# Queries and B's keys turned on VectorE in 32x32 blocks over all 128 rows, and carried between partition quarters by DMA

## The reference

```python
for l in range(DEPTH):                      # 2 layers
    x = x + 0.5 * _swiglu(_rmsnorm(x, ffn1_norm[l]), ...)
    h = _rmsnorm(x, mix_norm[l])
    a_q, a_kv, i_q, i_k, i_w, b_qkv, c_q, c_kv, c_g, m_g = jnp.split(h @ w_in[l], cuts, axis=-1)
    # rope on a_q, a_k, i_q, i_k, b_q, b_k, c_q (also used unrotated), k_slc, k_win
    # A: attention over the keys picked by the indexer (i_q, i_k, i_w)
    # B: causal attention with own keys for each of its 4 heads
    # C: 8 heads in 2 groups: compressed, selected (S) and window (W) attention, gated
    # the three branches, gated by m_g, are summed and go through w_out
    x = x + 0.5 * _swiglu(_rmsnorm(x, ffn2_norm[l]), ...)
return _rmsnorm(x, final_norm)
```

## Time and profile before

| | |
|---|---|
| median of 3 runs | 1163.5 us (1162.96 to 1163.73) |
| the profiled execution | 1163.91 us |
| its span, first to last instruction | 1162.2 us |
| TensorE busy | 1153.9 us (99% of the span) |
| VectorE busy | 951.5 us (82%) |
| ScalarE busy | 581.7 us (50%) |
| GpSimd busy | 31.9 us (3%) |
| turns on TensorE, line 1546 | 68 |
| block turns on VectorE, line 693 | 64, 19.4 us |
| granted TensorE clock | 0.998 of full speed |

### The profile page before, as it was taken

One profiled execution on the slowest core, in us unless ns is written; L12 is line 12 of the kernel. 1 busy time (PEld: TensorE's weight loads), 2 busy tenths in 40 slices (PEclk: granted clock), 3 DMA queues, 4 the chain that ended last, 5 costly groups with the idle time before them and its releaser, 6 DMA issues.

```text
span 1162.2 us, 16328 instructions
## 1 busy us (share of the span) xinstructions
PE 1153.9 (99%) x5573; PEld 945.9 (81%) x5573; DVE 951.5 (82%) x1788; ACT 581.7 (50%) x757; POOL 31.9 (3%) x67
## 2 busy tenths in 40 slices
PE   9999999999999999999999999999999999999997
PEld 7888888887778888888888888888877788888886
DVE  6877788899977687778887887878999696888777
ACT  6444345447764464344454444454578635434433
POOL 2000000001000000000000000000010000000000
PEclk9999999999999999999999999999999999999999
DMA  8566554765425555655556556556653335655561
GB/s 285 190 214 216 181 188 163 234 203 163 137 80 182 181 157 204 217 191 185 195 177 202 180 173 215 182 189 191 198 180 110 141 135 184 219 181 169 202 234 38
DMA packets 148996, 211.04 MB, mean 182 GB/s; under 512 B 8160, under 2 KB 109136, under 8 KB 148944
## 3 DMA queue, kind: packets, MB, share of 16 engines
q1 hardware_dynamic: 148256, 209.64, 54.5%
q10 hardware_dynamic: 688, 0.71, 0.2%
HBM read 209.28 MB, written 1.05 MB: 181 GB/s over the span
## 4 chain that ended last, share of the span: by engine, by line
PE 99%; DVE 0%; issue 0%; ACT 0%; POOLq 0%; POOL 0%; DVEq 0%
PE ps L1371 30%; PE ps L1373 30%; PE ps L1372 30%; PE ps L1585 2%; PE ps L1421 1%; PE ps L1641 1%; PE ps L1613 1%; PE ps L1390 1%; PE ps L1546 1%; PE ps L1558 0%; PE ps L1765 0%; PE ps L1672 0%; PE ps L1632 0%; DVE x L1000 0%; PE ps L1573 0%
## 5 line engine op out<-in xcount | busy, mean ns | idle before, releaser
L1114 ACT ACTIVATE whi<-raw 128x2048 fp32r<-128x2048 f32 (+1 forms) x195 | 365.9, 1879 | 253.3 <-PE ps L1373 252.2
L536 DVE TENSOR_TENSOR wlo<-raw,whi 128x2048 fp32r<-128x2048 f32 (+1 forms) x195 | 433.9, 2244 | 65.6 <-ACT whi L1114 45.7
L1371 PE MATMUL ps<-whi,ht_hi 128*128 128x512 f32 (+1 forms) x1192 | 465.6, 391 | 0.2
L1373 PE MATMUL ps<-whi,ht_lo 128*128 128x512 f32 (+1 forms) x1192 | 460.8, 387 | 0.0
L1372 PE MATMUL ps<-wlo,ht_hi 128*128 128x512 f32 (+1 forms) x1192 | 460.3, 386 | 0.0
L1373 PEld LDWEIGHTS ps<-whi,ht_lo 128*128 128x128 f32 x1192 | 223.9, 188 | 45.9
L1371 PEld LDWEIGHTS ps<-whi,ht_hi 128*128 128x128 f32 x1192 | 224.0, 188 | 45.0 <-issue 1.4
L1372 PEld LDWEIGHTS ps<-wlo,ht_hi 128*128 128x128 f32 x1192 | 224.1, 188 | 43.9
L598 DVE STREAM_TRANSPOSE scr<-scr 32x128 f32<-32x128 f32 x688 | 208.3, 303 | 10.3
L1371 PE MATMUL ps<-whi,at_hi 128*128 128x512 f32 x304 | 118.5, 390 | 0.0
L1372 PE MATMUL ps<-wlo,at_hi 128*128 128x512 f32 x304 | 118.3, 389 | 0.0
(11 more groups left out here) (176 smaller groups left out, 757.3 us busy)
## 6 DMA issues: line engine op xcount, KB each, us to landing
raw<-in_ffn_w_down_dram SPq DMA_DIRECT2D x88, 512.0 KB, 4.9
raw<-in_w_in_dram SPq DMA_DIRECT2D x88, 512.0 KB, 4.5
raw<-in_ffn_w_gate_dram SPq DMA_DIRECT2D x85, 512.0 KB, 4.0
raw<-in_ffn_w_up_dram SPq DMA_DIRECT2D x85, 512.0 KB, 5.0
raw<-in_w_out_dram SPq DMA_DIRECT2D x16, 512.0 KB, 4.4
raw<-in_w_branch_c_dram SPq DMA_DIRECT2D x8, 512.0 KB, 4.4
raw<-in_w_branch_b_dram SPq DMA_DIRECT2D x4, 512.0 KB, 3.9
raw<-in_w_branch_a_dram SPq DMA_DIRECT2D x4, 512.0 KB, 4.0
```

What stands on the lines that cost most here:

```text
L536: nc.vector.tensor_tensor(wlo[:, n, 0:w], raw[:, n, 0:w], whi[:, n, 0:w].bitcast(F32), ALU.subtract).then_inc(lo_done, 1)
L1114: nc.scalar.activation(whi[:, n, 0:w], raw[:, n, 0:w], ACT.Copy).then_inc(hi_done, 1)
L1371: nc.tensor.matmul(o, xh, wh, start=start, stop=False)
L1373: return nc.tensor.matmul(o, xl, wh, start=False, stop=stop)
```

## The change

The scores now read their queries, and B's keys, from tiles in which one token's value of 8 blocks x 2 token halves lie side by side, so that neighbouring tokens of a block are 16 numbers (64 bytes) apart in a row. VectorE turns 32 x 32 blocks within each quarter of 32 partitions, over all 128 rows at a time: 2 instructions of 128 x 1024 (the queries of A, I and B, and the keys of B) and 8 of 128 x 256 (C's queries, rotated and not). Then GpSimd asks for 16 transfers for each of the two sets, of 32 partitions x 2048 bytes, which carry every block to the quarter in which it belongs (`qk_1`, and `qk_2` in `gr`). TensorE keeps three fills for keys and two for the compressed branch. The scaling of the queries by `ATT_SCALE` moves into operations that are there anyway.

```diff
-FILLS = [((0, 1), "qs", 0), ((2,), "pair", 0), ((6, 7), "qs", 4),
-         ((14,), "pair", 4), ((15,), "pair", 6), ((10, 11), "qs", 6), ((12, 13), "qs", 8),
-         ((16, 17), "n", 0), ((18, 19), "n", 2)]
+FILLS = [((0,), 0), ((1,), 2), ((2,), 4)]
 NFILL = len(FILLS) + 2
-T1 = 3
-DVE_TURNS = {"I": (3, "q", 2), "K": (8, "k", 2)}
+T1 = 1
...
+        rs_1 = gr[:, 4096:6144].rearrange("p (t b c) -> p t b c", t=NT, b=NTURN)
+        qk_2 = gr[:, 4096:6144].rearrange("p (c b t) -> p c b t", b=NTURN, t=NT)
+        qk_1 = sb("qk_1", [P, SEQ // NT, NTURN, NT])
...
+        def queries(row, b, t):
+            return qk_1[row, :, b, t] if b < NTURN else qk_2[row, :, b - NTURN, t]
+        def keys(row, pair, kb, j, nt):
+            if pair == "B":
+                return qk_1[row, :, BKEYS + j, 0:nt].rearrange("p c t -> p t c")
+            return k_t[row, kb, 0:nt * P]
...
-                for a in range(*rows, 32):
-                    for q in range(0, P, 32):
-                        step(nc.vector.transpose(into[q:q + 32, :, :, a:a + 32], rs[a:a + 32, :, b:b + 2, q:q + 32]))
+                for t in range(NT):
+                    parts = [(0, rs_1[:, t])] if n == 0 else [(0, rs_2[:, t]), (4, pr[:, t, C_Q:C_Q + 512].rearrange(
+                        "p (b c) -> p b c", b=4))]
+                    for b0, src in parts:
+                        nb = src.shape[1]
+                        for q0, into in [(0, turned_1)] if n == 0 else [(0, turned_2[0]), (2, turned_2[1])]:
+                            nq = into.shape[1]
+                            dst = into.rearrange("p q (c b t) -> p q b t c", b=NTURN, t=NT)
+                            step(nc.vector.transpose(dst[:, :, b0:b0 + nb, t, :],
+                                                     src.rearrange("p b (q c) -> p q b c", q=4)[:, q0:q0 + nq]), ("turn", n))
...
-                step(nc.vector.memset(cmpm[:, :, :, :], 0.0), ("cmpm zero",))
...
-                    if m == 7:
-                        turn_blocks(l, "K", (0, 64))
-                    if m == 9:
-                        turn_blocks(l, "K", (64, P))
+                    if m == 8:
+                        turn_blocks(l, 0)
...
-                        turn_blocks(l, "I")
+                        turn_blocks(l, 1)
...
                 convert(l, S + 14)
+                dve.wait_ge(crossed[0], (l + 1) * 256)
+                step(nc.vector.memset(cmpm[:, :, :, :], 0.0), ("cmpm zero",))
...
+            def cross(l, n):
+                wait_step(pool, l, ("turn", n))
+                for a in range(4):
+                    for q in range(4):
+                        dst = (qk_1, qk_2)[n][32 * q:32 * q + 32, 32 * a:32 * a + 32, :, :].rearrange("p c b t -> p (c b t)")
+                        pool.dma_start(dst, turned_blocks(n, q)[32 * a:32 * a + 32]).then_inc(crossed[n], 16)
...
                 norm(l * 3 + 1)
+                cross(l, 0)
+                cross(l, 1)
...
+                if e < 2:
+                    pe.wait_ge(crossed[e], (l + 1) * 256)
...
-                    ins = nc.tensor.matmul(score_head(t, h), q_t[row, qb + h // 2, t * P:(t + 1) * P],
-                                           k_t[row, kb + kstep * (h // 2), 0:nk], start=opens, stop=n >= 6,
+                    ins = nc.tensor.matmul(score_head(t, h), queries(row, qb + h // 2, t),
+                                           keys(row, pair, kb, h // 2, t + 1), start=opens, stop=n >= 6,
...
-                for m in (13, 14):
-                    load_halves(l, S + m, w_in, 512 * (m - 13), 4, M_G, 512)
-                for q in range(2, 12):
-                    if q == 5:
-
-                        sp.wait_ge(fill_ps, (l + 1) * NFILL)
+                for q in range(12):
+                    if q == 2:
+                        sp.wait_ge(crossed[0], (l + 1) * 256)
                         sp.dma_start(w1[0][1], rows_cols(cmp_w1_k, l, 8 * P, 8, 0, P)).then_inc(w1_in[0], 16)
                     load_halves(l, S + 13 + q, w_in, 512 * (q % 2), 4, M_G + 512 * (q // 2), 512)
```

More of the change, by code:

```diff
@@ L65 @@
 M_B, M_A, M_C = 25, 26, 27
-QBLK = {"A": 0, "I": 2, "B": 4, "R": 6}
-KBLK = {"A": 0, "I": 1, "B": 2, "S": 4, "W": 6}
-NQB, NKB, NRB = 10, 8, 16
+QBLK = {"A": 0, "I": 2, "B": 4}
+KBLK = {"A": 0, "I": 1, "S": 2, "W": 4}
+BKEYS, NTURN, NKB, NPAIR = 6, 8, 6, 3
 ROPE = {
[L74 to L79, removed]
-}
-FILLS = [((0, 1), "qs", 0), ((2,), "pair", 0), ((6, 7), "qs", 4),
-         ((14,), "pair", 4), ((15,), "pair", 6), ((10, 11), "qs", 6), ((12, 13), "qs", 8),
-         ((16, 17), "n", 0), ((18, 19), "n", 2)]
+    0: [(A_Q, 4, ("first", 0)), (A_K, 1, ("pair", 0, 0))],
+    1: [(I_Q, 4, ("first", 2)), (I_K, 1, ("pair", 0, 1)), (B_Q, 4, ("first", 4))],
+    2: [(B_K, 4, ("first", BKEYS))],
+    3: [(C_Q, 8, ("second", 0))],
+    4: [(C_KS, 2, ("pair", 1))],
+    5: [(C_KW, 2, ("pair", 2))],
+}
+FILLS = [((0,), 0), ((1,), 2), ((2,), 4)]
 NFILL = len(FILLS) + 2
-T1 = 3
-DVE_TURNS = {"I": (3, "q", 2), "K": (8, "k", 2)}
+T1 = 1
 def by_act(f):
@@ L127 @@
 LAST_ORDER = [0, 2, 1, 3]
-V_STEPS = 277
+V_STEPS = 249
 SETUP_WARM, SETUP_G = 1, 19
@@ L180, in build, with turned_blocks @@
         sc_t = w1_k[:, SEQ:2 * SEQ]
-        qn_t = prob[:, 1, 512:1536].rearrange("p (b c) -> p b c", b=4)
+        turned_2 = [v.rearrange("p (q c) -> p q c", q=2) for v in (prob_all[:, 2048:3072], turned_x[:, :])]
+        def turned_blocks(n, q):
+            return turned_1[:, q, :] if n == 0 else turned_2[q // 2][:, q % 2, :]
         cos_s = sb("cos_s", [P, NT, HD])
@@ L273, in build @@
         fill_a = sem("fill_a")
+        crossed = [sem(f"crossed{n}") for n in range(2)]
         v_step = sem("v_step")
@@ L474, in copy_fill @@
                 return
[L475 to L482, removed]
+            b = FILLS[f][1]
+            for g in range(2):
+                for half in range(2):
+                    copy(k_t[half * HD:(half + 1) * HD, b + g, :], ps[g * HD:(g + 1) * HD, bank, 0:SEQ], 1.0)
         def load_x(eng, n):
@@ L660, in rope @@
                 dve.wait_ge(proj_done, l * 12 + 2 * u + 2)
-                for c0, nh, b0, part in ROPE[u]:
+                for c0, nh, place in ROPE[u]:
                     src = pr[:, :, c0:c0 + nh * HD].rearrange("p t (h c) -> p t h c", h=nh)
+                    into, b0 = {"first": rs_1, "second": rs_2, "pair": pairs}[place[0]], place[1]
                     if nh == 1:
-                        dst = rs[:, :, b0:b0 + 1, part * HD:part * HD + HD]
+                        dst = into[:, :, b0:b0 + 1, place[2] * HD:place[2] * HD + HD]
                     else:
-                        dst = rs[:, :, b0:b0 + nh // 2, :].rearrange("p t b (e c) -> p t (b e) c", e=2)
+                        dst = into[:, :, b0:b0 + nh // 2, :].rearrange("p t b (e c) -> p t (b e) c", e=2)
                     tmp = rtmp[:, :, 0:nh, :]
@@ L684, in fill_out, with turn_blocks @@
                 at_step["fill", f] = count[0]
[L686 to L689 removed]
+            def turn_blocks(l, n):
                 own(l)
[L691 to L693 removed]
+                for t in range(NT):
[8 more added lines that the diff above has]
+                                                     src.rearrange("p b (q c) -> p q b c", q=4)[:, q0:q0 + nq]), ("turn", n))
             def cmp_windows(l):
@@ L1539, in fill @@
                         if f < len(FILLS):
-                            b = FILLS[f][0][j]
-                            src = rs[:, t, b, :] if b < NRB else \
-                                pr[:, t, C_Q + (b - NRB) * P:C_Q + (b - NRB + 1) * P]
+                            src = pairs[:, t, FILLS[f][0][j], :]
                         else:
@@ L1568, in scores @@
                     wait_step(pe, l, ("max", e - 1, 1))
-                qb, kb, kstep, _, _ = heads_of(pair) if pair != "C" else (0,) * 5
+                if e < 2:
+                    pe.wait_ge(crossed[e], (l + 1) * 256)
+                qb, kb, _ = heads_of(pair) if pair != "C" else (0,) * 3
                 if pair == "C":
@@ L1633, in weighted @@
                                          start=j == 0, stop=False, skip_group_check=True)
-                opens, vcol = pair in "AB", heads_of(pair)[3]
+                opens, vcol = pair in "AB", heads_of(pair)[2]
                 for kt in range(NT):
@@ L1712, in compressed @@
                                      stop=True).then_inc(cmp_ps, 1)
-                wait_step(pe, l, ("fill", T1 + 4))
+                wait_step(pe, l, ("fill", NFILL - 2))
                 pe.wait_ge(fill_a, (l + 1) * NACT)
```

30 lines of the change are left out of this document (16 added, 14 removed).

## The result

The changed kernel takes 1175.38 us (median of 3 runs, 1175.14 to 1176.96) against 1163.5 before: ratio 1.0106, 95% interval 1.0087 to 1.0126. The forecast was slower, 1170.5; the time is 1.4 us above its upper bound of 1174. The profiled execution took 1175.14 us, its span 1173.4, at a granted clock of 0.998, as before. So the span grew by 11.2 us.

What follows compares the result with a forecast made beforehand. TensorE was taken to bound the kernel. Per layer -2.66 us (turns removed), +1.0 (wait for windows) and +5.2 (strided reads) gave +3.5, for two layers +7: 1163.5 + 7 = 1170.5 us, range 1159 to 1174.

Steps and rivals of the forecast that it cites:

- What bounds the kernel, and the sign: Whole kernel: TensorE holds 99% of the chain, VectorE 0%; only TensorE's work or waits move the end; slower 0.58, faster 0.31.
- The wide turns on VectorE: VectorE's turns of queries and keys: 5.8 to 8.4 us a layer instead of 10.6, costing nothing on the chain.
- The transfers: GpSimd's 16 requests per set at 1.0 us each, landing in 3 us; second set covered by 7 us, cost nothing.
- VectorE up to the windows: VectorE ahead of compress: windows end at 263.75, TensorE waits about 0.9 us; 1.0 us a layer given back, bounds 0 and 1.5.
- the late second set: Rival at pair C: at 1.4 us a request the set lands 6 us late; 1172 us, or 1182 with slow reads; chance 0.11.
- What is removed: TensorE's fills: 24 turns a layer go, 2.66 us, 0.89 ahead of slab 13 and 1.77 ahead of slab 14, all on the chain.
- Queries and keys 64 bytes apart: TensorE's scores: strided reads at 1.7 ns a column add 5.2 us a layer, bounds 0 and 5.2; the deciding term.
- at its old pace: Rival on the scores: TensorE reads the stride as fast as before; 1160.2 us, or 1158.2 without the windows' wait; chance 0.31.
- in between: Rival on the scores: the stride costs about 1.2 ns a column, gain and loss cancel, 1163.5 us; chance 0.08.

## Why the prediction was wrong, step by step

- **What bounds the kernel, and the sign**: right. TensorE's own reading decided, by the term that I had named as the one that decides.
- **The wide turns on VectorE**: right. 7.5 us a layer, inside 5.8 to 8.4, nearer the upper end, hidden.
- **The transfers**: right in effect. I took 1.0 us for a request, between 0.44 and 1.4; it was 0.50. A landing took 2.9 us for the first set, forecast 3, and some 6 for the second, which I had put at 3 too: 3 us of the 7 of cover. TensorE waited for neither, so the late second set is refuted. VectorE did not hold a request up: its slabs and turns ran beside them, and of the 64 the longest took 0.73 us.
- **VectorE up to the windows**: right in the mechanism, and within 0.4 us. That the end of the windows agrees to 0.01 us is luck: this execution's mixer began 0.4 us earlier than the one I had reckoned from, and the windows came 0.4 us later than forecast when counted from the first fill. Part of it is ScalarE's copy in four pieces: 1.54 us instead of 1.08, where I had added 0.3. The wait was 0.6 to 0.7 us instead of about 1.0, because TensorE came there later still, for the next reason.
- **What is removed**: this step failed. "24 turns ... All on the chain" took the earlier trace rows for the first group as time won. The ten turns from 250.20 to 251.55 covered VectorE's convert of slab 13, which ended at about the same moment. The run with three turns shows it: 0.78 us taken away, 0.86 us waited. From the first fill to slab 13 it was 1.35 us before and 1.36 after: the eight turns there brought nothing of the 0.89 us that I had put to them, because of a gate that I had not looked for. The sixteen behind slab 13 brought 1.9, so of 2.66 us a layer 1.91 came. The earlier trace rows held a hint: ten turns in 1.35 us are 0.135 each, against 0.111 in the second group.
- **Queries and keys 64 bytes apart**: the mechanism was right, and one term of the sum was mis-sized. The price of a column was right (1.7 ns), partly by luck: I took VectorE's whole price of a column, and that the two engines' bases (1.03 and 0.8 ns) and surcharges (0.64 and 0.92) add up alike, nothing here explains. Right were also B (2.87 us, forecast 2.83) and nearly C (+0.53, forecast +0.44). The six other pairs were forecast at +0.56 and measured +0.75. I had modelled a pair as nine loads in a row, 1.96 us; the row has 2.26. The same model gave 1.40 for a pair before, where the chain has 1.51; what it leaves out grew from 0.11 to 0.30 us. The traces show the place. The loads of a row group start 0.22 us apart, as forecast, except at the load that carries the wait inside the pair (`odd_done`, head 0): it starts 0.53 us behind the one that stands before it in its group (266.33 and 266.87 in pair I; which group a load belongs to is inferred from the starts). It is so in all six pairs of both layers, and in the kernel before with the stride alone. That is 0.3 us for each pair where the wait cost 0.1 before, and by it +0.56 became +0.75. Over six pairs and two layers the miss is 2.3 us.
- **What the sum lacked**: the end of the program. GpSimd's longer drain costs 1.2 us, and neither the sum nor a rival had it.

From the forecast of +7.1 to the measured +11.2: +2.4 for the scores, +1.5 for the turns, -0.6 for the windows' wait, +1.2 for the drain, -0.4 at the start, which is not the change's. The upper end of the range was missed by 1.4 us: with the scores or the turns forecast right the time would have lain inside, with the drain alone not quite. The rival "at its old pace" was refuted (it asked for loads at 186 ns; they are 304), "in between" too. The upper end of the range held only the cases I had priced, with no allowance for a term that none of them had.

## What to carry to other kernels

A layout that suits the engine that writes a tile is paid for by the engine that reads it, here by the only one that is always busy: keep float32 numbers that TensorE reads one after another no more than 8 bytes apart, in weights as in moving operands. The same change with the axes of its two tiles in another order is 0.15% faster than before instead of 1.1% slower, and 0.26% with the memset in an idle place.

Work taken off the bounding engine counts only down to what the other engines deliver at that point. Before a saving is put into a sum, look up when the next operand's producer ends, in front of that very place; where the two end together, as here at 251.4, the saving is nothing.

A queue's engine has prices beside the transfer: the request (0.50 to 0.61 us each here), what is asked for behind it, and the end of the program. A long wait of TensorE has one too: the products behind 3.9 to 4.4 us of standing ran at half the clock for some 3 us.

## What the runs showed of the hardware

- TensorE reads float32 at full pace with a step of 4 or 8 bytes, and at about half with 64 (a load each 0.22 us instead of 0.11), with loads as long or longer at 16 and 32, as weights (186, 192, 322, 328, 304 ns for 64 rows by 128 columns) and as the moving operand (391, 400, 624, 632, 662 ns for 256 columns of C). That 64 bytes make loads cheaper than 32, and the moving operand of C dearer, was not explained.
- VectorE's block turns of 128 x 1024 take 1.22 us when they write with a step of 8 bytes and 1.98 with 64.
- A transfer from SBUF to SBUF of 32 rows by 2 KB costs GpSimd 0.50 us to ask for and lands after 5.0 us (median of 64; 2.9 for the first set of a layer, about 6 for the second); in stretches of 256 bytes it is 0.58 and 5.1 us; asked for by SP in such stretches it costs 0.61 us to ask for.
- When TensorE had stood for 4.4 and 3.9 us, the granted clock of the next stretch was 0.50, the lower level of 1.2 GHz, and products of 128 x 512 started 0.43 us apart instead of 0.23. Behind the waits of 1.0 us at the gate it stayed at 1.00.
- The drain of GpSimd at the end of the program took 0.66 us without transfers of its own, 0.76 with one, 5.9 with 64, and 2.0 with 64 in stretches of 256 bytes.
